# GpSimd's high part of each weight unit: an addition of zero replaced by a converting copy, in a two-block transformer kernel

## What is computed

```
# first block, per layer
h = x @ w_in[l]
out_a = causal softmax attention with forget gates      # "fox"
out_b = multi-head latent attention                     # "mla"
out_c = stick-breaking attention                        # "stick"
out_d = sliding-window attention with sinks             # "swa"
y = _group_rmsnorm(mix, mix_g[l]) @ w_o[l]
x = _layernorm(ALPHA * x + y, ln1_g[l], ln1_b[l])
f = (jax.nn.silu(x @ w_gate[l]) * (x @ w_up[l])) @ w_down[l]
x = _layernorm(ALPHA * x + f, ln2_g[l], ln2_b[l])

# second block, per layer
h = x + 0.5 * swiglu(rms_norm(x, ffn1_norm[l]), ...)
y_da  = diff_attention(...)                             # differential attention
y_sc  = sc_b * causal_dwconv(sc_c * sc_x, sc_conv_w[l])
y_lru = jax.nn.gelu(lru_g) * rg_lru(xr, ...)            # gated linear recurrence
h = h + concatenate([y_da, y_sc, y_lru]) @ w_out[l]
x = h + 0.5 * swiglu(rms_norm(h, ffn2_norm[l]), ...)
return rms_norm(x, final_norm)
```

## Time and profile before

| what | value |
| --- | --- |
| median of 3 runs | 3571.46 us (3567.9 to 3572.3) |
| the profiled execution's own time | 3568.88 us |
| its span (first to last instruction) | 3567.1 us |
| mean granted TensorE clock | 0.959 of full speed |
| busy: PE, PEld, DVE, ACT, POOL | 3407.6, 2632.4, 1596.3, 696.4, 2344.9 us |
| DMA queue of the weights | 275.81 MB, 80 GB/s mean over the span for all queues |

### The profile page before, as it was taken

How to read it: one execution, slowest core, us unless ns; L and a number is a source line. 1 busy time by engine, 2 the same in 40 slices (tenths; PEclk the granted TensorE clock), 3 DMA queues, 4 the chain that set the end, 5 groups by cost and what they waited for, 6 DMA issues and landing times.

```text
span 3567.1 us, 41977 instructions
## 1 busy us (share of the span) xinstructions
PE 3407.6 (96%) x14430; PEld 2632.4 (74%) x14430; DVE 1596.3 (45%) x1864; ACT 696.4 (20%) x1380; POOL 2344.9 (66%) x1046
## 2 busy tenths in 40 slices
PE   8999899989998999979999989999999999899998
PEld 6755688868655788858888757888888887578886
DVE  4554311135455211155533776553355328765532
ACT  2252211012341210031110232111111101321110
POOL 6601577757304677748887736887788877468874
PEclk9997899989878999989999989999999999999999
DMA  4200222223101222212223212222222223122221
GB/s 158 82 1 18 66 93 94 94 72 107 42 1 48 77 94 92 93 53 93 94 94 109 89 48 72 94 94 94 96 94 93 94 92 108 54 71 92 92 94 64
DMA packets 82012, 286.31 MB, mean 80 GB/s; under 512 B 9531, under 2 KB 13020, under 8 KB 81628
## 3 DMA queue, kind: packets, MB, share of 16 engines
q1 hardware_dynamic: 76032, 275.81, 23.1%
q10 hardware_dynamic: 5852, 8.78, 0.8%
HBM read 280.89 MB, written 3.67 MB: 80 GB/s over the span
## 4 chain that ended last, share of the span: by engine, by line
PE 68%; DVE 4%; issue 2%; ACT 1%; DVEq 0%; ACTq 0%
PE bank_v L329 14%; PE bank_v L331 14%; PE bank_v L330 14%; PE bank_a L329 7%; PE bank_a L330 7%; PE bank_a L331 7%; PE bank_v L463 2%; PE bank_a L439 1%; PE bank_s L368 1%; PE bank_s L376 1%; PE bank_s L550 0%; PE bank_s L534 0%; DVE lru_x L1439 0%; PE bank_s L519 0%; DVE lru_x L1446 0%
## 5 line engine op out<-in xcount | busy, mean ns | idle before, releaser
L301 POOL TENSOR_TENSOR w_hi<-raw,zero 128x1024 fp32r<-128x1024 f32 x520 | 995.2, 1914 | 1145.7 <-PE bank_v L331 888.3
L304 POOL TENSOR_TENSOR w_lo<-raw,w_hi 128x1024 fp32r<-128x1024 f32 x520 | 1349.8, 2596 | 40.9
L329 PE MATMUL bank_v<-xn_hi,w_hi 128*128 128x512 f32 x1408 | 565.9, 402 | 15.3 <-DVE xn_lo L1024 15.3
L329 PE MATMUL bank_a<-xn_hi,w_hi 128*128 128x512 f32 x1360 | 543.9, 400 | 24.7 <-DVE xn_lo L1086 15.1
L330 PE MATMUL bank_v<-xn_lo,w_hi 128*128 128x512 f32 x1408 | 559.3, 397 | 0.0
L331 PE MATMUL bank_v<-xn_hi,w_lo 128*128 128x512 f32 x1408 | 559.2, 397 | 0.0
L330 PE MATMUL bank_a<-xn_lo,w_hi 128*128 128x512 f32 x1360 | 539.8, 397 | 0.0
L331 PE MATMUL bank_a<-xn_hi,w_lo 128*128 128x512 f32 x1360 | 539.4, 397 | 0.0
L331 PE MATMUL bank_v<-h_hi,w_lo 128*128 128x512 f32 x1056 | 417.7, 396 | 0.0
L329 PE MATMUL bank_v<-h_hi,w_hi 128*128 128x512 f32 x1056 | 417.6, 396 | 0.0
L330 PE MATMUL bank_v<-h_lo,w_hi 128*128 128x512 f32 x1056 | 417.6, 396 | 0.0
(11 more groups left out here) (290 smaller groups left out, 3626.7 us busy)
## 6 DMA issues: line engine op xcount, KB each, us to landing
raw<-in_w_stream SPq DMA_DIRECT2D x520, 512.0 KB, 3.3
rope<-in_rope ACTq DMA_DIRECT2D x2, 1024.0 KB, 5.8
da_v<-t_rows ACTq DMA_DIRECT2D x2, 1024.0 KB, 6.4
out<-resid SPq DMA_DIRECT2D x4, 512.0 KB, 2.7
t_rows<-t_row ACTq DMA_DIRECT2D x1, 1536.0 KB, 7.3
resid<-in_x SPq DMA_DIRECT2D x4, 256.0 KB, 3.7
resid<-in_x ACTq DMA_DIRECT2D x4, 256.0 KB, 8.7
mla_v<-in_alibi ACTq DMA_DIRECT2D x2, 512.0 KB, 6.6
```

The lines of the kernel that those rows point to most:

```text
L301: pool.tensor_tensor(w_hi[:, u, :], raw[:, u, :], zero[:, 0:1].to_broadcast([P, UNIT]), ALU.add).then_inc(*hi_split.done(("unit", u)))
L304: pool.tensor_tensor(w_lo[:, u, :], raw[:, u, :], w_hi[:, u, :].bitcast(F32), ALU.subtract).then_inc(*w_split.done(("unit", u)))
L329: pe.matmul(out, lhs_hi, rhs_hi, start=first, stop=False)
```

## The change

The addition of zero that makes `w_hi` becomes a converting copy with one input. The wait for the slot (`w_used`) stood on the addition; it now stands on a new addition of one column, `zero2 = zero + zero`, which nothing reads. The copy follows it in POOL's queue.

```
--- before.py
+++ after.py
@@ -179,6 +179,7 @@
         zero = sb("zero", [P, 1])
+        zero2 = sb("zero2", [P, 1])
         par1 = sb("par1", [P, N1])
@@ -298,8 +299,8 @@
                     pool.wait_ge(w_used.sem, w_split.before(("unit", u))[1])
-                    pool.tensor_tensor(w_hi[:, u, :], raw[:, u, :], zero[:, 0:1].to_broadcast([P, UNIT]),
-                                       ALU.add).then_inc(*hi_split.done(("unit", u)))
+                    pool.tensor_tensor(zero2[:, :], zero[:, :], zero[:, :], ALU.add)
+                    pool.tensor_copy(w_hi[:, u, :], raw[:, u, :]).then_inc(*hi_split.done(("unit", u)))
                     pool.wait_ge(*hi_split.after(("unit", u)))
                     pool.tensor_tensor(w_lo[:, u, :], raw[:, u, :], w_hi[:, u, :].bitcast(F32),
                                        ALU.subtract).then_inc(*w_split.done(("unit", u)))
```

## The result

| | before | changed |
| --- | --- | --- |
| median | 3569.68 us (3566.17 to 3572.3, 4 runs) | 3467.4 us (3457.33 to 3472.65, 4 runs) |
| ratio | | 0.9711 [0.9685, 0.9736] |
| the profiled execution's own time | 3568.88 us | 3464.11 us |
| its span and mean granted clock | 3567.1 us, 0.959 | 3462.3 us, 0.961 |

The kernel became 102 us faster, 2.9%. The forecast was 15.5 us, with 3546 as the lower end: the sign was right, the size was not. Lines behind the new allocation have moved by one.

The account below looks back on a forecast made before the run. The prediction took PE as the bound, with POOL paced by it, gains coming only where PE waits for DVE behind POOL. Terms of 2.8 + 2.8 + 2.9 + 7.0 = 15.5 us took 3571.5 to 3556.0 us, range 3546 to 3573.

Parts of the forecast that it names:

- What bounds the kernel: Whole kernel: PE is the bound, busy 96% of the span; POOL is paced by PE in the feed-forward loops.
- Everything else is costed at nothing: Feed-forward loops: PE's 5.6 us per unit cover POOL's 4.3 to 4.7, so no gain there.
- Rivals 1 and 3: First: copy costs about the addition, 3571 us, chance 0.13. Third: slow copy makes POOL the bound, 3586 to 4020, 0.13.
- The four terms: PE's waits at start, layernorms, before first attention and in second block's recurrence: 2.8 + 2.8 + 2.9 + 7.0 = 15.5 us.
- Start: POOL's first filling of four slots: four shorter `w_hi` turns let PE run on 2.8 us earlier.
- Layernorms: Four layernorms: running sum L1072 ends 0.69 us earlier behind POOL's `w_hi`, and PE's wait with it, 2.8 us.
- Before the first attention: Four additions L1321 meet POOL less, so PE's whole wait on L1205 goes, 2.9 us.
- Recurrence: Second block, twice: DVE meets shorter `w_hi` turns, row maxima that release PE come 3.5 us earlier, 7.0 us together.
- Rival 2: Copy fast but half the gain lost: DVE meets `w_lo` in recurrence, attention may get another clock; 3566 us, chance 0.12.

Follow-up runs that it names:

- e1_place_only: Kernel before plus an unused `zero2`, moving every tensor behind it 32 bytes further, POOL's instructions unchanged: 3491.42 us, ratio 0.9777.
- e9_both_off: Kernel before with weights moved 32 bytes and activations 64, so their distance is a multiple of 256: 3494.86 us, ratio 0.9795.
- e2: The copy alone: changed kernel with a second column of `zero` replacing `zero2`, so no tensor moves against the kernel before: 3536.83 us, ratio 0.989.
- e7: Changed kernel with 128 bytes of padding more before the activations: 3529.12 us, ratio 0.9878 to the kernel before.
- e4: Changed kernel with 64 bytes of padding more before the activations: 3490.73 us, ratio 0.9772 to the kernel before.
- m3_fine: A kernel of matmuls alone on constant data, other engines idle, with operand starts shifted by distances finer than 32 bytes: 719.5 us.

## Why the prediction was wrong

**What bounds the kernel: right.** PE was the bound and is it still, and POOL waits for PE in the feed-forward loops. POOL's idle time rose by 373 us with the copy alone (1145.7 to 1519.1), where 350 had been forecast, and by 292 in the changed kernel, whose faster PE leaves POOL less of it. The inference "a faster POOL moves no matmul there" holds too: the copy alone leaves 387 matmuls in 90 us.

**The step that failed: "Everything else is costed at nothing",** and with it "the feed-forward stretches unchanged at 388 matmuls per 90 us". The change has three parts, and the prediction priced two. The third is the line of the diff that allocates `zero2`. It was taken as free, since nothing reads the tensor; but it moved the activations by 32 bytes against the weights, and the start-to-start time of 12048 matmuls from 233.3 to 226.7 ns. That is some 80 us of the 102, which agrees with what the place alone measured (83 in `e1_place_only`, 77 in `e9_both_off`). No rival had it either; all three were about what POOL's instructions cost.

**The copy: right.** Taken at 1.05 us, measured 1.056 in the mean and 1.04 where it meets nobody. The Trainium skill ("GPSIMD Engine Reference", Elementwise — side-by-side cycle accounting) has 1.03 and about 1.8 cycles per element, from which the prediction estimated 0.98 and 1.64 us; the trace is near the first. Rivals 1 and 3, which needed a slow copy, are out. That a one-input copy blocks DVE for its own duration, as the addition did, holds too. DVE and POOL in the changed kernel, at the instruction of the earlier trace rows:

```profile
362.06 1.04 DVE L1073 TENSOR_TENSOR work<-work,resid 128x512 f32<-128x512 f32 x1
...
361.52 1.04 POOL L303 CAST w_hi<-raw 128x1024 fp32r<-128x1024 f32 x1
```

The copy ends at 362.56 and L1073 at 363.10, 0.54 later, where it had been 0.55 behind the addition.

**The one-column addition: its duration too low, its cost right.** It was expected near 100 ns and its rows show 222 in the mean (190 to 200 when alone). But the copy starts 0.14 us after it, where 0.15 had been taken. From its start to the copy's end a `w_hi` turn is 1.18 us (forecast 1.20), as POOL's timeline of the changed kernel shows, beside the earlier trace rows:

```profile
604.57 0.20 POOL L302 TENSOR_TENSOR zero<-zero 128x1 f32<-128x1 f32 x1 [1.79 <-PE bank_v L332]
604.71 1.04 POOL L303 CAST w_hi<-raw 128x1024 fp32r<-128x1024 f32 x1
605.83 2.40 POOL L305 TENSOR_TENSOR w_lo<-raw,w_hi 128x1024 fp32r<-128x1024 f32 x1
```

**The four terms: right in their sum and mostly in their places.** Forecast 15.5 us; PE's waits fell by 18.1 in the changed kernel and by 19.9 with the copy alone.

- Start, forecast 2.8. POOL's last filling instruction ended at 29.09 before, at 25.77 with the copy alone and at 27.20 in the changed kernel: 3.3 and 1.9 earlier. With the copy alone 0.45 of it is the first load, which landed sooner. PE's wait of L329 on L1024 fell by 3.9 and by 2.6.
- Layernorms, forecast 2.8: the wait of L392 on L1072 fell from 10.3 to 7.4, so 2.9.
- Before the first attention, forecast 2.9: that wait is gone, in both kernels with the copy. The four additions took 7.79 us and now take 3.22, where 4.6 had been forecast; this is their row in DVE's timeline of the changed kernel:

```profile
151.67 3.22 DVE L1322 TENSOR_TENSOR mla_q<-mla_q,work 32x512 f32<-32x512 f32 x4
```

- Recurrence, forecast 7.0: the wait for ACT's probs fell from 15.1 to 5.3 (4.6 with the copy alone), so 10 us. This term was a third too small: with a turn of 1.18 instead of 1.89 more of DVE's instructions miss POOL altogether. The running sum shows how many. Its median went from 2881 ns to 680, which is its time without a collision:

```profile
L1073 DVE TENSOR_TENSOR work<-work x49: 677/680/2878, 1529.1 to 3447.6; 128x512 f32<-128x512 f32 x49
```

**What the copy gave beyond the waits.** The copy alone gained 37 us in the medians, 20 of them waits. In the two profiled executions, which were granted nearly the same clock (0.961 and 0.959), it gained 24.5, so there the waits are most of it. Rival 2 had named the place of the rest, "may be granted another clock", with the wrong sign. The stretches from the start of the first layers' attention to the next unit, kernel before (the number after POOL is the granted clock, here the mean over a stretch that has both levels, 1.2 and 2.4 GHz):

```profile
146.70:360.20 213.50, 196.96 (x740) 118.84 (x741) 116.35 (x255) 79.69 (x224) 35.62 (x17) 0.85 0.07 22
913.10:1127.60 214.50, 199.57 (x740) 119.84 (x741) 116.34 (x255) 79.60 (x224) 35.63 (x16) 0.83 0.07 22
```

and the same two with the copy alone:

```profile
141.90:346.80 204.90, 190.26 (x741) 116.25 (x740) 111.11 (x256) 79.40 (x224) 29.93 (x25) 0.88 0.07 24
897.80:1117.70 219.90, 205.41 (x740) 123.43 (x739) 111.33 (x256) 79.67 (x224) 29.95 (x25) 0.81 0.07 22
```

The same work takes 204.9 us at 0.88 and 219.9 at 0.81: one stage gained 8.6 and the other lost 5.4. The mean granted clock of whole runs was 0.9635, 0.9635, 0.9605 and 0.9595 (`e2`, `e7`, `e4`, changed kernel, four runs each) with the copy, and 0.9547 to 0.9592 in the seven kernels with the addition. At the 2.4 to 3 us per 0.001 seen between runs, the 0.0057 between the kernel before and `e2` are 14 to 17 us, and 20 of waits with them make the 37. For the changed kernel, with 0.9595 against 0.9578, it is 4 to 5 us: 80 + 18 + 5 = 103, against 102 measured. A higher mean clock goes with the copy in `e2` and `e7` (single runs 0.959 to 0.967, against 0.955 to 0.962 in 33 runs of the kernel before). The changed kernel's four runs (0.957 to 0.962) lie within those of the kernel before, so that for it the share of the clock is not shown. By what way the copy would bring a higher clock stays open.

**What else stays open.** Why a distance that is no multiple of 256 bytes costs PE 6.6 ns of 227 was not found; the runs show that it does, not what in the chip does it. Nor was it found why the rate at other distances also depends on something else, as in `e7_after_128_more` and `m3_fine`. A wait placed on the copy itself, without the one-column addition, wasn't tried.

## What to carry to other kernels

An allocation is an edit: before a small change is called a gain, time the kernel before with the same tensors at the same addresses, since here some 80 of 102 us had nothing to do with the instruction that was changed. In a kernel bound by matmuls, look at where the moving and the stationary operand start; a distance that is a multiple of 256 bytes gave 2.2% here for an unused tensor that takes 32 bytes. And when PE's busy time falls while its count of matmuls and its clock do not, the cause lies in the matmuls, not in what they wait for.

## What the hardware showed that was not expected

- Three-pass float32r matmuls of 128x512 start every 226.7 ns when stationary and moving operand start a multiple of 256 bytes apart, 228.9 at 64 bytes more, 232.4 or 233.3 at 128, 233.3 at 32 and 224. At multiples of 256 it did not matter where either operand itself started (0, 32, 64, 96 and 128 bytes were tried), nor whether POOL was busy. Matmuls of 384 columns did not gain.
- A GpSimd copy from float32 to float32r of 128x1024 takes 1.04 us, the addition of a repeated zero column with the same output 1.89, a difference of two tensors 2.39, an addition of one column 0.19 to 0.22.
- The same attention stage of this kernel takes 204.9 to 219.9 us as the clock granted to it goes from 0.88 to 0.81.
